# Conditioning blocks behind the prompt attention's heads, one dense block per sample batch, first tile's values on three engines

## The reference, cut to what matters

```python
def trunk_layer(x, c, pos, lw, st, mla_past):
    mod = jax.nn.silu(c) @ lw['w_ada'] + lw['b_ada']
    sh1, sc1, g1, sh2, sc2, g2 = jnp.split(mod[:, None, :], 6, axis=-1)
    u = x * (1.0 + sc1) + sh1
    mix, new_st = mixer_branches(u, pos, lw, st, mla_past)
    x = layer_norm(DEEPNORM_ALPHA * x + g1 * mix, lw['ln1_g'], lw['ln1_b'])
    u2 = x * (1.0 + sc2) + sh2
    f = (jax.nn.silu(u2 @ lw['w1']) * (u2 @ lw['w3'])) @ lw['w2']
    x = layer_norm(DEEPNORM_ALPHA * x + g2 * f, lw['ln2_g'], lw['ln2_b'])
    return x, new_st
```

## Time and profile before

| | |
|---|---|
| median of 3 runs | 1873.16 us (1868.24 to 1875.08) |
| the profiled execution's own time | 1869.28 us |
| its span, first to last instruction | 1867.3 us |
| TensorE (PE) busy | 1706.9 us, 91% |
| VectorE (DVE), ScalarE (ACT), GpSimd (POOL) busy | 806.9, 735.0, 700.8 us |
| DMA, mean over the span | 166 GB/s |
| mean granted TensorE clock | 0.960 of 2.4 GHz |

### The profile page before, as it was taken

The page is one execution under the profiler, slowest core; times in us unless marked ns, Lnnn a source line. Parts: engine busy times, 40 slices in busy tenths (PEclk is TensorE's granted clock), DMA queues, the critical chain, the costliest instruction groups (busy, mean ns, idle before and its releaser), DMA issues.

```text
span 1867.3 us, 30317 instructions
## 1 busy us (share of the span) xinstructions
PE 1706.9 (91%) x10994; PEld 1470.4 (79%) x10994; DVE 806.9 (43%) x1887; ACT 735.0 (39%) x1110; POOL 700.8 (38%) x438
## 2 busy tenths in 40 slices
PE   3899999999799989999838999999997999899997
PEld 1788899886477869999717888998864778799996
DVE  0445386655331353332314544876553223533233
ACT  1455534334333244442314564442333432444332
POOL 0434555544122423333113445564531234233331
PEclk9899999999899989999968999999998999899999
DMA  9243335248765344443072523362587643434440
GB/s 352 97 177 114 102 108 204 91 164 305 282 228 201 118 181 149 145 159 135 29 287 91 188 92 102 111 215 85 176 313 281 240 171 127 183 141 157 148 145 29
DMA packets 73246, 309.10 MB, mean 166 GB/s; under 512 B 15554, under 2 KB 25090, under 8 KB 43010
## 3 DMA queue, kind: packets, MB, share of 16 engines
q1 hardware_dynamic: 73090, 307.09, 45.8%
HBM read 291.81 MB, written 15.25 MB: 164 GB/s over the span
## 4 chain that ended last, share of the span: by engine, by line
PE 39%; DVE 6%; DMA 2%; issue 1%; ACT 1%; SPq 1%; DVEq 0%; ACTq 0%
PE zps L429 5%; PE zps L434 5%; PE zps L430 4%; PE zps L890 4%; PE zps L891 4%; PE zps L892 4%; PE zps L413 4%; DMA ring<-wpack_dram 1%; PE mps L736 1%; PE mps L413 1%; DVE arena L1689 1%; PE mps L760 1%; DMA arena<-cache_dram 1%; PE zps L463 1%; PE mps L641 1%
## 5 line engine op out<-in xcount | busy, mean ns | idle before, releaser
L2015 POOL TENSOR_TENSOR wlx<-ring,wh 128x1024 fp32r<-128x1024 f32 x172 | 409.3, 2379 | 708.1 <-ACT wh L1046 702.2
L429 PE MATMUL zps<-uhi,wh 128*128 128x320 f32 x1232 | 380.4, 321 | 1.8 <-ACT wh L1046 1.7
L430 PE MATMUL zps<-ulo,wh 128*128 128x320 f32 x1232 | 367.7, 311 | 0.0
L1046 ACT ACTIVATE wh<-ring 128x1024 fp32r<-128x1024 f32 x172 | 182.3, 1060 | 356.2 <-PE zps L430 252.7
L2115 POOL TENSOR_TENSOR wlo<-ring,whi 128x1024 fp32r<-128x1024 f32 x66 | 160.2, 2427 | 311.2 <-ACT whi L1046 310.3
L429 PEld LDWEIGHTS zps<-uhi,wh 128*128 128x128 f32 x1232 | 235.0, 191 | 14.4 <-issue 9.2
L430 PEld LDWEIGHTS zps<-ulo,wh 128*128 128x128 f32 x1232 | 235.0, 191 | 0.8
L890 PE MATMUL zps<-xhi,whi 128*128 128x320 f32 x688 | 213.8, 311 | 0.0
L891 PE MATMUL zps<-xlo,whi 128*128 128x320 f32 x688 | 213.3, 310 | 0.0
L892 PE MATMUL zps<-xhi,wlo 128*128 128x320 f32 x688 | 213.2, 310 | 0.0
L434 PE MATMUL zps<-uhi,wlx 128*128 128x320 f32 x1248 | 210.5, 311 | 0.0
(11 more groups left out here) (279 smaller groups left out, 2548.6 us busy)
## 6 DMA issues: line engine op xcount, KB each, us to landing
ring<-wpack_dram SPq DMA_DIRECT2D x222, 1024.0 KB, 4.9
arena<-cache_dram SPq DMA_DIRECT2D x128, 320.0 KB, 4.9
arena<-stateA_dram SPq DMA_DIRECT2D x2, 2064.0 KB, 9.7
o_cn_s<-arena SPq DMA_DIRECT2D x2, 2064.0 KB, 11.2
arena<-stateD_dram SPq DMA_DIRECT2D x2, 2048.0 KB, 11.9
o_ret_s<-arena SPq DMA_DIRECT2D x2, 2048.0 KB, 11.6
x<-o_y SPq DMA_DIRECT2D x2, 1280.0 KB, 10.1
o_y<-x SPq DMA_DIRECT2D x4, 640.0 KB, 3.0
```

Of the source, the lines that this page charges most:

```text
L429: nc.tensor.matmul(o, hi[:, k * P:(k + 1) * P], xh[:, k, :], start=k == 0, stop=False)
L430: last = nc.tensor.matmul(o, hi[:, k * P:(k + 1) * P], xl[:, k, :], start=False, stop=False)
L1046: return nc.scalar.activation(out, in_, func, **kw).then_inc(*ev(sem, label))
L2015: G().tensor_tensor(wlx[:, n % RING, half], ring[:, n % RING, half], wh[:, i, :], ALU.subtract).then_inc(*ev("pool_l", (q, i)))
```

## The change

It has four parts. First, ada 8 to 15 leave the slots: one stands behind each of the first seven heads of the prompt attention, one behind the first convolution block. Second, the slots hold one dense block for each batch and at most one ada; the two other steps of batch b move into its own slot, the transposes between the block's two tiles and the values behind it, and the convolution's norm moves from slot 3 to slot 1. Third, the first tile of a layer: ScalarE makes `uhi` straight from x, VectorE makes prompt tiles 0 to 3 in PSUM and the samples in `taps_ps`, GpSimd makes tiles 4 to 7, and the tile's products stand in another order (`opening_tile`). Fourth, the taps are dealt anew: all of VectorE's must be done by the norm in slot 1.

```diff
+          + [b for k, (x, i) in enumerate(A_STREAM) for b in (("in", f"{x}{i}", f"{x}{i + 1}"), ("ada", 8 + k))]
+          + [("in", "cg0", "ca0"), ("ada", 15)] + [("in", f"cg{j}", f"ca{j}") for j in range(1, 4)]
-SLOTS = [[("gate", 2, 0)],
-         [("ada", 8), ("gate", 2, 2), ("ada", 9)],
-         [("ada", 10), ("ada", 11), ("ada", 12)],
-         [("ada", 13), ("ada", 14), ("ada", 15)],
-         [("branch", 2, 0), ("gate", 2, 4), ("ada", 16)],
-         [("gate", 2, 6), ("branch", 2, 4), ("ada", 17)],
-         [("gate", 1, 0), ("gate", 1, 2)],
-         [("gate", 1, 4), ("ada", 18)],
-         [("gate", 1, 6), ("ada", 19)]]
-CONV_NORM = 3
+SLOTS = [[("gate", 2, 0)], [("gate", 2, 2)], [("branch", 2, 0)], [("gate", 2, 4), ("ada", 16)], [("gate", 2, 6), ("ada", 17)],
+         [("branch", 2, 4), ("ada", 18)], [("gate", 1, 0), ("ada", 19)], [("gate", 1, 2)], [("gate", 1, 4)]]
+CONV_NORM = 1
+BLOCKS += [("in", "g1_6", "g1_7")]
...
-        uhi, ulo = over("uhi", [P, KC, T], "x"), over("ulo", [P, KC, T], "u")
+        uhi, ulo = over("uhi", [P, KC, T], "u"), over("ulo", [P, KC, T], "x")
...
+                    def opening_tile(q, n, name, freed_by):
+                        o, hi = bank("z", name, freed_by)[:, 0:T], wh[:, 0, :]
+                        pe.wait_ge(*at("act_hq", (q, 0)))
+                        pe.wait_ge(*at("act_uh", "samples"))
+                        pe.wait_ge(*at("pool_l", (q, 0)))
+                        for k in range(KC):
+                            pe.wait_ge(*at("act_uh", k))
+                            nc.tensor.matmul(o, hi[:, k * P:(k + 1) * P], uhi[:, k, :], start=k == 0, stop=False)
+                            nc.tensor.matmul(o, wlx[:, n % RING, k * P:(k + 1) * P], uhi[:, k, :], start=False, stop=False)
+                        pe.wait_ge(*at("dve_ul", "samples"))
+                        for k in range(KC):
+                            pe.wait_ge(*at("dve_ul", k))
+                            last = nc.tensor.matmul(o, hi[:, k * P:(k + 1) * P], ulo[:, k, :], start=False, stop=k == KC - 1)
...
+                    for b in range(NB + 1):
+                        if b < NB:
+                            sample_scores(b)
                         if b == CONV_NORM:
                             pe.wait_ge(*at("pool_c", ("sum", CW - 1)))
                             channel_sum("conv sum", y[:, 2], 4, ("dve_c", ("tap", 3, CW - 1)), ("dve_c", ("mu", 3)))
+                        slot(b, in_the_middle(b), at_the_end(b))
+                    gate(1, 6)
                     branch(1, 0)
...
-                            if n == SLOT_START[b - 1] + RING - 1:
+                            if n == SLOT_START[b - 2] + RING + (b == NB - 1):
                                 load_pages(b)
...
-                    high(0)
-                    act.wait_ge(pre["pre_dma"], 80)
+                    high(0, (0,))
+                    act.wait_ge(*at("dve_u", "sc"))
                     for k in range(KC):
-                        act.wait_ge(*at("dve_u", ("p", k)))
-                        go("act_uh", k, uhi[:, k, :], u[:, k, :], ACT.Copy)
+                        go("act_uh", k, uhi[:, k, 0:SEQ], x[:, k, 0:SEQ], ACT.Identity, bias=mod[:, k, 0:1], scale=mod[:, KC + k, 0:1])
+                        if k == 0:
+                            act.wait_ge(*at("dve_u", "s2"))
+                            go("act_uh", "samples", uhi[:, :, SAMP], taps_ps[:, :].rearrange("p (k t) -> p k t", k=KC), ACT.Copy)
+                    high(0, (1,))
...
+                        def prompt(k):
+                            return mps[k][:, 0:SEQ] if k < KC // 2 else acc[:, k, 0:SEQ]
+                        for k in range(KC // 2):
+                            V().tensor_scalar(prompt(k), x[:, k, 0:SEQ], sc[:, k, 0:1], sh[:, k, 0:1], ALU.mult, ALU.add).then_inc(*ev("dve_u", ("p", k)))
...
+                            V().tensor_tensor(ulo[:, k, 0:SEQ], prompt(k), uhi[:, k, 0:SEQ], ALU.subtract).then_inc(*ev("dve_ul", k))
...
-                    gated(3, 0, behind=1)
-                    taps(14)
-                    gated(3, 4, behind=2)
+                    gated(3, 0, behind=3)
+                    taps(22)
+                    gated(3, 4, behind=4)
...
+                    low_of("small", 0)
+                    pool.wait_ge(*at("dve_u", "sc"))
+                    for k in range(KC // 2, KC):
+                        G().tensor_scalar(acc[:, k, 0:SEQ], x[:, k, 0:SEQ], mod[:, KC + k, 0:1], mod[:, k, 0:1], ALU.mult, ALU.add).then_inc(*ev("pool_u", k))
+                    low_of("small", 1)
```

179 lines of the change are left out of this document (95 added, 84 removed).

## The result

The changed kernel takes 1854.11 us (median of 11 runs, 1847.27 to 1862.36), the kernel before 1869.12 in the same series (11 runs, 1865.79 to 1875.45). The ratio is 0.9915, with an interval of 0.9894 to 0.9935: faster by 15 us, where 40.0 were forecast. The profiled execution took 1859.16 us at a span of 1857.5, so it is 5 us above its median, and the two profiles stand only 10 us apart, less than the two medians.

A forecast was written before the change was run, and what follows sets the result against it. TensorE, busy nine tenths of the span, was the bound: only idle time and clock winnable. 2 x 13.8 + 5.9 + 6.5 = 40.0 off 1869.3 gave 1829.3 profiled; forecast 1831, range 1816 to beyond 1854.

The forecast's parts named there:

- I count no wait: Heads: next input block lands about 5 us into an iteration of about 10.3, halves ready before use, so no wait.
- the wait for the silus: Slots, before branch (2, 0): silus said to be ready just when TensorE wants them, so nothing was added.
- the term for the clock: Slots: slow products behind the 2.5 us wait at the convolution's sum, between 0 and 3, taken as 1.5 us.
- late softmax: Slots: softmax fits by 1.1 us, costed at nothing in slots 1 to 7; rival, late in each slot: 1885, chance 0.05.
- the wait at the sum: Slot 1: TensorE waits for the convolution norm's sum, held by GpSimd's last three taps behind block g2_2: +2.5 us.
- where 0.5 was counted: Slot 0: VectorE comes late to the softmax and the margin of `sample_back` is lacking: +0.5 us.
- the first cache wait: Slots: the first wait for the cache, 0.4 us, was predicted to stay.
- the 0.7 of batch 7: Slots: batch 7's pages stand behind one block more, since it waits for ada 18: +0.7 us.
- the 1.5 us that were to hide behind head 6: Heads: ada 14 and a turn fill TensorE's 1.32 us wait for an m bank behind head 6: -1.5 us.
- not before 9 us: Heads: ScalarE's exponentials, behind its wait for the late input block, are not needed before 9 us into the iteration.
- one last difference is caught: Opening: two or three of VectorE's last differences slip behind GpSimd's second low half; without it 1.9 us shorter per layer.
- the late loads: Rival in the slots: weights or pages come late, a layer gives back 8 to 10 us: 1850, chance 0.13.

The follow-up runs named there:

- the last experiment: Changed kernel with tiles first behind the heads, sums in PSUM, taps ahead, later GpSimd low halves, ada 15 in slot 3, silus before g2_4's second high half: 1819.04 us.
- sums in PSUM: Changed kernel with VectorE putting the sums of an ada pair into unused columns of their m bank in PSUM instead of into mod in SBUF: 1848.83 us.
- spare products: Changed kernel with extra TensorE products in the opening whose sums nobody reads: 1853.25 us, ratio 0.9912 to the kernel before.
- The repairs: Edits on the changed kernel: tiles first behind the heads, sums in PSUM, taps ahead, later low halves, ada 15 in slot 3, silus before a high half; together 1819.04 us.
- taps ahead: Changed kernel with GpSimd's last three convolution taps ahead of the low halves of block g2_2 instead of behind them: 1846.57 us, ratio 0.9870 to the kernel before.

## Why the prediction was wrong

The direction was right, the size was not: 15 us of the 40. Three steps carry most of the loss. "I count no wait" at the heads was wrong. Ada 15 was counted at its products alone, where it brought a wait and slower work. And in the slots the wait for the silus was put at nothing and the term for the clock was too small.

- **Slots, predicted 148.2, measured 152.1 and 153.0.** Right: no wait for the cache behind the first slot, no late softmax in most slots, and the wait at the sum, 2.63 us for a predicted 2.5. Wrong is the sentence that the silus are ready "just when branch (2, 0) wants them". ScalarE makes a high half ahead of them, and TensorE waits 1.63 us; the last experiment shows it. Two further waits stand at the transposes in each layer, 0.5 to 0.9 us each, one of them in slot 0, where 0.5 was counted, one in slot 6, where none was. Of the 4.1 us of idle time that the sum adds, 0.4 (the first cache wait) ends just as the stretch begins and so lies outside it, and the 0.7 of batch 7 did not come. In all TensorE is idle for 5.6 and 5.7 us. The term for the clock, 1.5, was too small in this profile: TensorE is busy for 146.5 and 147.3 us, and in the last kernel, at a clock of 1.00 and with one ada of 1.07 more, for 144.3. By these numbers I estimate the slow products at 3.3 and 4.1 us. In three other kernels with the same slots (old opening, sums in PSUM, spare products) it is busy for 145.1, which gives 1.9. No kernel with these slots came under 150.2 us, so the miss is not chance alone. And the price of the alternative was too low: I took 9.5 us out of the slots for eight adas, where the run that puts them back pays 24 to 28.
- **Heads, predicted +7.0, measured +10.8 in both layers.** The blocks' own price was right: TensorE's busy time there is 65.2 us in the last kernel and 56.5 in the one with the adas back in the slots, both at a clock of 1.00, so 8.6 for a predicted 8.5. The failed step is "I count no wait", with the 1.5 us that were to hide behind head 6. The prediction did list what stands behind the late block on ScalarE (a tile's bank, the exponentials), but let the exponentials come "not before 9 us". That is so for a head with an input block behind it. Behind head 6 there is none: TensorE had made its scores at 186.4 us and wanted a bank for head 7's at 189.3, which ScalarE frees behind its exponentials, and the wait grew from 1.32 to 2.02. VectorE's addition in a turn, caught by a low half of GpSimd, was not in the sum at all: 1.54 and 1.58 us of waiting at head 3. So idle time rose by 2.0 and 1.5 us where it should have fallen by 1.3. How often the addition is caught differs from run to run, but no kernel with these heads came under 68.7 us.
- **Convolution to slots, predicted +1.0 a layer, measured +4.0 and +5.0.** Ada 15 was costed at its products. Without it the stretch is that of before. By the windows 1.4 and 1.5 us of the difference are idle time, of which 0.85 and 1.11 are a wait for ScalarE's last prompt output, which stands behind ada 15's copy. The other 2.6 and 3.5 are busy time: 1.1 of it ada 15's own, and the rest, by estimate, slower products.
- **Opening, predicted -5.9 and -6.5, measured -3.9 and -6.6.** In both layers one last difference is caught, as predicted (2.41 us for 0.42). In layer 1 GpSimd's first low half also met VectorE's bias addition (2.07 us for 0.20). I had placed that half by the block's landing, but costed the operations on `mod` beside it at their free price. Which layer is hit is chance: from the same opening other profiles have 12.4 and 12.6 in the two layers, or 14.4 to 14.5 in both, so that the good number of layer 2 was partly luck.
- **Behind the opening, predicted 0, measured +3.9 in all.** The work is unchanged; the granted clock was 0.91 and 0.97 against 0.94 and 0.97 in the kernel before. In the other kernels of these runs the same stretch took 60.2 to 62.0 us, once 63.9. Why it was slower here stays open: kernels with the same opening have it at 60.3 as well, and spare products did not move the median.

The forecast of 1831 had a small slip of its own: 1829.3 and 3.9 make 1833.2. And the 3.9 came from a median of three; over 11 runs the median of the kernel before is 1869.12, the time of its profiled execution.

Of the rivals, the late loads came nearest by time (1850), but not by mechanism as it was priced, in waits of the sample batches: no page was late. What was late was a weight block for ScalarE, with other work behind it.

## What to carry to other kernels

When a block is moved so that its successor lands later, list what stands behind the first instruction that waits for it on each engine, not only when TensorE wants it: a high half of ScalarE ahead of a ready tile, ahead of silus or ahead of a copy cost TensorE 1 to 20 us here. When VectorE and GpSimd share a stretch, give their start an order by a wait of its own; a wait on the same event for both, or none, leaves 2 us to a start 0.02 us earlier, and it falls differently from layer to layer and from run to run. The repairs took out half a dozen waits of 1 to 2.6 us in each layer and were worth 35 us together; by profile about half of that is idle time, and the rest is work of TensorE that ran faster. And before a microsecond or two in one profiled stretch is put down to an edit, look at the same stretch in kernels where it was not edited.

## What the runs showed of the hardware

- VectorE stood still for the length of a GpSimd low half (2.34 us) not only with two tensors in SBUF: an addition of 1.0 to 128x72 within SBUF took 2.18 us instead of 0.20. A scale and shift of 128x256 from SBUF into PSUM took 0.55 us in every new opening, beside GpSimd or not.
- A lead of 0.02 to 0.03 us decided who waited (960.97 against 960.99, 151.69 against 151.72).
- In the slots the granted clock was 0.94 and 0.93 with 16 to 18 us of idle time (adas in the slots), 0.96 with 12.4 (before), 0.98 and 0.97 with 5.6 (the change), 0.99 with 3.7 and 4.5 (taps ahead), 1.00 with 1.4 and 2.3 (the last). More idle time of TensorE went with a lower clock, and so cost more than its length; but not strictly, since with sums in PSUM 5.5 us of idle time went with 0.99.
